# The shared expert's fifth token tile ahead of the routed loop, and ScalarE makes the statistics of three tiles of the second norm

## The chip, the cores and the metric

The kernel runs on one core of one Trainium2 chip. A core has TensorE (PE, matmuls), VectorE (DVE), ScalarE (ACT) and GpSimd (POOL), and SyncE (SP), which issues DMAs; the engines run their own instruction streams and meet by semaphores. The metric is the time of one execution on the device in microseconds; several executions are timed and the median counts.

## What is computed

One layer of a decoder trunk for 1024 tokens of width 1024: a token mixer with four branches, a layer norm, a mixture of experts, a second layer norm. The change touches the shared expert of the mixture and the second norm.

```python
def layer_norm(x, g, b):
    mu = jnp.mean(xf, -1, keepdims=True)
    var = jnp.mean(jnp.square(xf - mu), -1, keepdims=True)
    return ((xf - mu) * lax.rsqrt(var + LN_EPS) * g + b).astype(x.dtype)
...
# moe_ffn: 64 experts of width 256, 6 of them per token, rows sorted by expert in blocks of 128
h = xpad[tok]
y = (jax.nn.silu(h @ wg[e]) * (h @ wu[e])) @ wd[e]
...
shared = (jax.nn.silu(xt @ sh_wg) * (xt @ sh_wu)) @ sh_wd
x = layer_norm(ALPHA * x + (routed + shared), ln2_g, ln2_b)
```

## The kernel before

The tokens lie in NT = 8 tiles of 128 rows. The last half of the program (the function back) has three stages that matter here.

**Ahead of the routed loop.** The first norm makes x1 of every tile, TensorE turns it (turn_x1), the router is computed, and then TensorE makes the shared expert of the first NU = 4 tiles. For one tile t that is: shared_up(t), 8 matmuls of 128x512 for gate and up together; ScalarE's silu and a copy of the up half (shared_gated); GpSimd's product of both (shared_hidden, L1552); TensorE turns the product (shared_turn, L1663); ScalarE copies the turned product out (L1964); TensorE's shared_down (4 matmuls, L1672); ScalarE empties the banks (L1974); GpSimd adds ALPHA * x1 (L1582) and stores the sum as the tile's rows of acc in HBM (L1584). s_y counts the tiles whose banks are empty. SyncE waits for s_y to reach NU before it loads the weights of experts 2 and 3. The other tiles' rows of acc are ALPHA * x1 alone.

**The routed loop.** 76 blocks, each of up to 128 rows of one expert: gather by GpSimd, turn, up (L1704 and L1700 to L1702), down (L1719, 12 matmuls), and a scatter with addition to acc (even blocks) or acc_odd (odd blocks).

**The last stage.** Behind the last routed down product TensorE makes the shared expert of tiles 4 to 7 (shared_up at L1652, tail_turn at L1779, tail_down at L1790), one tile's up product ahead of the turn and down product of the tile before. ScalarE makes the silu (tail_gated, L1988) and copies the turned product (tail_turned, L1993), VectorE the product (tail_hidden, L2282). SyncE reads the eight tiles of acc into SBUF (L1523), GpSimd reads acc_odd on top of them with an adding DMA (L1615), and odd_in[t] tells that tile t is complete. Then the second norm, tile by tile: for tiles 4 to 7 VectorE adds the shared expert's two halves from the banks (L2315, it counts s_y up); VectorE makes the statistics of the two halves (L2319) and puts them together (L2321); ScalarE takes the root (deviation, L2033); VectorE's three 128x1 instructions (scales, L2298 to L2300) make scale and shift; ScalarE applies them (normal, L2037); VectorE multiplies by the gain g2 (gain, L2304); GpSimd adds the offset b2 (L1619); SyncE stores the tile. tail_down(6) and (7) wait for the banks that VectorE's addition of tiles 4 and 5 empties. The order of all this on each engine is written out by hand; nothing schedules it.

## Time and profile before

| | us |
|---|---|
| median of 3 runs | 2075.33 |
| lowest and highest | 2073.94, 2077.75 |
| the profiled execution | 2077.22 |
| its span, first to last instruction | 2075.4 |

The profile is of one execution. Its page gives TensorE as busy for 2010.3 us (97% of the span), VectorE for 1350.9 (65%), ScalarE for 859.5 (41%), GpSimd for 553.1 (27%). The shares are means over stages with different limits; what one stage is worth is read from its own rows. A row of the timeline has the start, the duration, the engine, the line, what it writes and reads, and in brackets the idle time ahead and what ended it. The chain of waits follows the work that ended last back from the last instruction; its rows are start, duration, engine, tile and line.

### The profile page before, as it was taken

How to read it: one execution, taken by the hardware profiler on the slowest of the kernel's cores; microseconds unless marked ns; L12 is line 12 of the kernel's file. 1: busy time of each engine (PE TensorE's matmuls, PEld its weight loads, DVE VectorE, ACT ScalarE, POOL GpSimd, SP SyncE). 2: the span in 40 equal slices, each digit the busy share in tenths (PEclk: the TensorE clock that was granted, in tenths of full speed). 3: DMA queues.
4: the chain of work that ended last, by engine and by line, in shares of the span. 5: the costliest groups of instructions: out<-in, count | busy, mean ns of one | idle time of the engine just before them, and what ended most of it. 6: DMA issues, size and time to landing. Idle time of an engine off the chain costs nothing.

```text
span 2075.4 us, 33282 instructions
## 1 busy us (share of the span) xinstructions
PE 2010.3 (97%) x9805; PEld 1448.0 (70%) x9806; DVE 1350.9 (65%) x2797; ACT 859.5 (41%) x1446; POOL 553.1 (27%) x366
## 2 busy tenths in 40 slices
PE   8999999999999999989999999999999999999995
PEld 7887787877778766668667457666667776666762
DVE  2894543344026777788667657777777777777756
ACT  2111221344112344430133256656666666666643
POOL 2342231323322211012120132223222222332224
PEclk9999999999999999999999999999999999999998
DMA  6122221222622210158551488899898989899856
GB/s 199 51 67 92 76 61 31 82 56 62 168 66 82 64 47 27 43 202 294 195 226 44 171 323 292 309 350 337 319 327 277 358 292 331 311 312 305 298 169 184
DMA packets 167747, 389.07 MB, mean 187 GB/s; under 512 B 26193, under 2 KB 98162, under 8 KB 142961
## 3 DMA queue, kind: packets, MB, share of 16 engines
q1 hardware_dynamic: 129696, 298.02, 39.4%
q0 software_dynamic: 28752, 73.18, 14.1%
q10 hardware_dynamic: 9216, 16.78, 2.2%
q8 instruction: 50, 0.82, 0.2%
q14 instruction: 33, 0.26, 0.0%
HBM read 337.04 MB, written 80.22 MB: 201 GB/s over the span
## 4 chain that ended last, share of the span: by engine, by line
PE 40%; DMA 6%; issue 2%; DVE 2%; ACT 1%; ACTq 0%; DVEq 0%; POOLq 0%
PE e_bank L1704 9%; PE e_bank L1719 9%; DMA work<-x1d,idx 6%; PE e_bank L1682 3%; PE e_bank L1634 3%; PE e_bank L1700 3%; PE e_bank L1652 3%; PE e_bank L1701 2%; PE e_bank L1702 2%; PE e_bank L1644 2%; PE e_bank L1672 1%; PE e_bank L1753 1%; PE e_bank L1790 1%; PE e_bank L1853 1%; PE e_bank L1731 1%
## 5 line engine op out<-in xcount | busy, mean ns | idle before, releaser
L646 PE MATMUL a_bank<-x_hi,w_hi 128*128 128x512 f32 x928 | 373.2, 402 | 0.0
L646 PE MATMUL a_bank<-x_hi,w_lo 128*128 128x512 f32 x928 | 362.7, 391 | 0.0
L646 PE MATMUL a_bank<-x_lo,w_hi 128*128 128x512 f32 x928 | 361.8, 390 | 0.0
L1704 PE MATMUL e_bank<-w_gu,work 128*128 x616 | 277.2, 593 | 2.1 <-issue 1.4
L2236 DVE TENSOR_TENSOR d_lo<-w_d,d_hi 128x1024 fp32r<-128x1024 f32 x152 | 180.8, 1230 | 61.2 <-ACT d_hi L2001 61.1
L581 POOL CAST w_hi<-w_raw 128x1024 fp32r<-128x1024 f32 x56 | 64.7, 1156 | 560.2 <-PE a_bank L646 539.5
L646 PEld LDWEIGHTS a_bank<-x_hi,w_hi 128*128 128x128 f32 x928 | 174.4, 188 | 40.5 <-issue 6.1
L646 PEld LDWEIGHTS a_bank<-x_hi,w_lo 128*128 128x128 f32 x928 | 174.2, 188 | 37.7
L646 PEld LDWEIGHTS a_bank<-x_lo,w_hi 128*128 128x128 f32 x928 | 174.7, 188 | 33.9 <-issue 0.5
L1704 PEld LDWEIGHTS e_bank<-w_gu,work 128*128 128x128 f32 x616 | 111.9, 192 | 113.3 <-issue 113.3
L1900 ACT ACTIVATE u_hi<-w_gu 128x1024 fp32r x150 | 159.0, 1061 | 2.0 <-POOL work L1582 1.7
L2001 ACT ACTIVATE d_hi<-w_d 128x1024 fp32r x152 | 152.3, 1049 | 5.6 <-issue 3.7
L583 POOL TENSOR_TENSOR w_lo<-w_raw,w_hi 128x1024 fp32r<-128x1024 f32 x56 | 145.4, 2596 | 4.6
L1905 ACT ACTIVATE norm<-e_bank 128x256 f32<-128x256 f32 x76 | 29.2, 384 | 252.3 <-PE e_bank L1702 248.5
L1598 POOL DMA_INDIRECT acc<-work,idx_out x38 | 80.2, 2111 | 197.5 <-issue 191.3
L1542 POOL DMA_INDIRECT work<-x1d,idx x77 | 81.4, 1057 | 181.0 <-DVE idx L2201 169.6
L1598 POOL DMA_INDIRECT acc_odd<-work,idx_out x38 | 74.7, 1966 | 202.7 <-DVE idx_out L2257 189.2
L1719 PE MATMUL e_bank<-d_hi,h_hi 128*128 128x512 f32 x304 | 126.0, 414 | 0.0
L1700 PE MATMUL e_bank<-u_hi,x_g_hi 128*128 128x512 f32 x300 | 124.8, 416 | 0.0
L874 ACT ACTIVATE gate_out<-a_bank 128x512 f32<-128x512 f32 x64 | 38.2, 597 | 204.7 <-PE a_bank L646 204.5
L1719 PE MATMUL e_bank<-d_hi,h_lo 128*128 128x512 f32 x304 | 120.5, 397 | 0.0
L1719 PE MATMUL e_bank<-d_lo,h_hi 128*128 128x512 f32 x304 | 119.3, 392 | 0.0
(378 smaller groups left out, 3867.1 us busy)
## 6 DMA issues: line engine op xcount, KB each, us to landing
w_gu<-in_moe_wg SPq DMA_DIRECT2D x64, 1024.0 KB
w_gu<-in_moe_wu SPq DMA_DIRECT2D x64, 1024.0 KB
w_d<-in_moe_wd SPq DMA_DIRECT2D x64, 1024.0 KB, 12.5
w_raw<-in_w_in SPq DMA_DIRECT2D x53, 512.0 KB, 3.8
gates<-gate_out ACTq DMA_DIRECT2D x64, 256.0 KB, 2.0
g_sb<-gates SPq DMA_DIRECT2D x16, 1024.0 KB, 5.3
acc_odd<-zero POOLq DMA_DIRECT2D x9, 512.0 KB, 13.3
work<-in_w_out SPq DMA_DIRECT2D x4, 1024.0 KB, 8.8
```

Source lines behind the costliest of these rows:

```text
L581: pool.tensor_copy(w_hi[:, c % 2, :, :], w_raw[:, c % 2, :, :]).then_inc(w_hi_ready, 1)
L583: pool.tensor_tensor(w_lo[:, c % 2, :, :], w_raw[:, c % 2, :, :], w_hi[:, c % 2, :, :].bitcast(F32), ALU.subtract).then_inc(w_lo_ready, 1)
L646: ins = pe.matmul(bank[h][:, :], w[:, c % 2, k, :], x[:, k, cols], start=(k == 0 and j == 0), stop=(k == KD - 1 and j == 2))
L1542: pool.indirect_dma_start(out=x_g[:, s, :], out_offset=None, in_=x1d[:, :], in_offset=bass.IndirectOffsetOnAxis(ap=idx[:, s:s + 1], axis=0 ...
L1598: pool.indirect_dma_start(out=(acc, acc_odd)[s][:, :], out_offset=bass.IndirectOffsetOnAxis(ap=idx_out[:, s:s + 1], axis=0), in_=y_out[:, ...
L1634: pe.matmul(bank[2 * (t % 2) + h][:, :], merged[:, k, rows], w_out[:, k, h * HALF:(h + 1) * HALF], start=k == 0, stop=False)
L1700: pe.matmul(out, hi, u_hi[:, j, :, i, :], start=False, stop=False)
L1704: ins = pe.matmul(out, x_gt[:, s, k, :], w_gu[:, bass.ds(e & 3, 1), :, k, :].rearrange('p a m f -> p (a m) f'), start=k == 0, stop=k == KD ...
L1719: ins = pe.matmul(bank[2 + h][:, :], x[:, j, :], w[:, j, cols], start=j == 0 and i == 0, stop=j == 1 and i == 2)
L1900: act.activation(up_part(u_hi[:, j, :, :, :]), up_weights(slot, j), ACT.Copy).then_inc(u_hi_ready, 1)
L2001: act.activation(d_hi[:, j, :], w_d[:, bass.ds(e & 3, 1), j, :].rearrange('p a f -> p (a f)'), ACT.Copy).then_inc(d_hi_ready, 1)
L2236: dve.tensor_tensor(d_lo[:, j, :], w_d[:, bass.ds(slot, 1), j, :].rearrange('p a f -> p (a f)'), d_hi[:, j, :].bitcast(F32), ALU.subtract) ...
```

## The change

NM = 5 tiles now have their shared expert made ahead of the routed loop, and the last stage has it for tiles 5 to 7. SyncE, ScalarE, GpSimd and TensorE go by NM where they went by NU; only tiles 5 to 7 have plain ALPHA * x1 rows in acc. In the second norm the tiles 0, 2 and 4 (BY_ACT) get their statistics from ScalarE: a copy of the tile onto itself with the row sums as a second output, VectorE makes the mean of it (one 128x1 instruction), and ScalarE squares the difference to the mean with the sums of squares as a second output (row_sums). The root takes those sums with a scale of 1/D. The other five tiles keep VectorE's statistics. The order of the last stage is new on TensorE, ScalarE and VectorE; the silu of tile 7 now stands ahead of all norms.

```diff
 NU = NT // 2
+NM = NU + 1
+BY_ACT = (0, 2, 4)
...
         m_lo = nc.alloc_sbuf_tensor_at('m_lo', [P, 4, S], F32R, offset=work_at + 4 * 4 * S)
+        squares = w_gu[:, 2, 0, 0:4, :].rearrange('p k f -> p (k f)')
         g2, b2 = (w_gu[:, 1, 1, 4 * i:4 * i + 4, :].rearrange('p k f -> p (k f)') for i in range(2))
...
         scale, shift = sb('ln2_scale', [P, NT]), sb('ln2_shift', [P, NT])
+        sums = sb('ln2_sums', [P, NT, 2])
+        row_sum, row_mean, squared = sem('row_sum'), sem('row_mean'), sem('squared')
...
             load_down(1, 1)
-            for t in range(NU, NT):
-                sp.wait_ge(x_scaled, t - NU + 1)
+            for t in range(NM, NT):
+                sp.wait_ge(x_scaled, t - NM + 1)
                 sp.dma_start(acc[t * P:(t + 1) * P, :], x1_n[:, t, :]).then_inc(acc_rest, 16)
...
             down_landed(0, 0)
-            sp.wait_ge(s_y, NU)
+            sp.wait_ge(s_y, NM)
             load_up(2, 2)
...
             load_down(3, 3)
-            sp.wait_ge(acc_rest, 16 * (NT - NU))
+            sp.wait_ge(acc_rest, 16 * (NT - NM))
             load_up(3, 3)
...
             shared_hidden(0)
-            for t in range(NU):
+            for t in range(NM):
                 s = t % 2
-                if t + 1 < NU:
+                if t + 1 < NM:
                     shared_hidden(t + 1)
...
             for s in range(2):
-                pool.wait_ge(acc_in[s], 16 * NU // 2)
-            pool.wait_ge(acc_rest, 16 * (NT - NU))
+                pool.wait_ge(acc_in[s], 16 * ((NM + 1 - s) // 2))
+            pool.wait_ge(acc_rest, 16 * (NT - NM))
             n = trips(pool)
...
                 for k in range(KD) if part is None else range(4 * part, 4 * part + 4):
-                    ins = pe.matmul(bank[s][:, :], turned_x1(t)[:, k, :], (s_gu if t < NU else tail_gu)[:, k, :], start=k == 0,
+                    ins = pe.matmul(bank[s][:, :], turned_x1(t)[:, k, :], (s_gu if t < NM else tail_gu)[:, k, :], start=k == 0,
                                     stop=k == KD - 1)
...
                 pe.wait_ge(s_ht_out, t + 1)
-                if t >= NU + 2:
+                if t >= NM + 2:
                     pe.wait_ge(s_y, t - 1)
...
             shared_turn(2)
+            shared_up(4)
             shared_down(2)
...
             shared_down(3)
-            pe.wait_ge(s_ht_out, NU)
+            shared_turn(4)
+            shared_down(4)
+            pe.wait_ge(s_ht_out, NM)
             turn(0, 0, 16)
...
                 up(0, 0, e_first[0], part)
-            pe.wait_ge(s_y, NU)
+            pe.wait_ge(s_y, NM)
...
                     pe.wait_ge(tail_in, 48)
-                    shared_up(NU)
+                    shared_up(NM)
                 if ahead1:
...
             body(2 * n + 1, 1, n, ahead1=False, ahead=False)
-            shared_up(5)
-            tail_turn(4)
-            pe.wait_ge(y_act, 2 * n + 3)
-            tail_down(4)
             shared_up(6)
             tail_turn(5)
+            pe.wait_ge(y_act, 2 * n + 3)
             tail_down(5)
...
             act.wait_ge(x1_stored, 16 * NT)
-            for t in range(NU):
+            for t in range(NM):
                 s = t % 2
...
                                ).then_inc(s_ht_out, 1)
-                if t + 1 < NU:
+                if t + 1 < NM:
                     shared_gated(t + 1)
-                act.activation(x1_n[:, NU + t, :], x1_n[:, NU + t, :], ACT.Copy, scale=ALPHA).then_inc(x_scaled, 1)
+                if t < NT - NM:
+                    act.activation(x1_n[:, NM + t, :], x1_n[:, NM + t, :], ACT.Copy, scale=ALPHA).then_inc(x_scaled, 1)
                 if t >= 2:
...
             e_one = expert_of(act, 1)
-            act.wait_ge(s_acc_ready, NU)
+            act.wait_ge(s_acc_ready, NM)
             act.wait_ge(gu_landed, e_one + 1)
...
                 else:
-                    tail_gated(NU)
+                    tail_gated(NM)
                 if ahead:
...
+            def row_sums(t):
+
+                act.wait_ge(odd_in[t], 16)
+                act.activation(rows2[:, t, :], rows2[:, t, :], ACT.Copy, accum_out=sums[:, t, 0:1]).then_inc(row_sum, 1)
+                act.wait_ge(row_mean, BY_ACT.index(t) + 1)
+                act.activation(squares, rows2[:, t, :], ACT.Square, scale=-1.0, bias=mv[:, t % 2, 0:1],
+                               accum_out=sums[:, t, 1:2]).then_inc(squared, 1)
+
             def deviation(t):
-                act.wait_ge(mv_done2, t + 1)
-                act.activation(sd[:, t % 2:t % 2 + 1], mv[:, t % 2, 1:2], ACT.Sqrt, bias=eps[:, 0:1]).then_inc(sd_done2, 1)
+                if t in BY_ACT:
+                    act.wait_ge(squared, BY_ACT.index(t) + 1)
+                    act.activation(sd[:, t % 2:t % 2 + 1], sums[:, t, 1:2], ACT.Sqrt, scale=1.0 / D, bias=eps[:, 0:1]
+                                   ).then_inc(sd_done2, 1)
+                else:
+                    act.wait_ge(mv_done2, sum(i not in BY_ACT for i in range(t + 1)))
+                    act.activation(sd[:, t % 2:t % 2 + 1], mv[:, t % 2, 1:2], ACT.Sqrt, bias=eps[:, 0:1]).then_inc(sd_done2, 1)
...
                                bias=shift[:, t:t + 1]).then_inc(normed, 1)
-            tail_gated(5)
-            tail_turned(4)
-            act.wait_ge(s_h, NU + 1)
             tail_gated(6)
             tail_turned(5)
+            act.wait_ge(s_h, NM + 1)
+            tail_gated(7)
+            tail_turned(6)
+            row_sums(0)
             deviation(0)
...
             normal(0)
+            act.wait_ge(s_down, NM + 1)
+            tail_turned(7)
+            normal(1)
+            row_sums(2)
             deviation(2)
-            normal(1)
             deviation(3)
             normal(2)
-            act.wait_ge(s_h, NU + 2)
-            tail_gated(7)
-            act.wait_ge(s_down, NU + 1)
-            tail_turned(6)
-            act.wait_ge(s_down, NU + 2)
-            tail_turned(7)
+            normal(3)
+            row_sums(4)
             for t in range(4, NT):
                 deviation(t)
-                normal(t - 1)
+                if t > 4:
+                    normal(t - 1)
             normal(NT - 1)
...
             body(2 * n + 1, 1, n, ahead1=False, ahead=False)
-            dve.wait_ge(ht_done, 2 * n + 3)
-            tail_hidden(4)
             dve.wait_ge(ht_done, 2 * n + 4)
             tail_hidden(5)
-            dve.wait_ge(s_ht, NU + 1)
             tail_hidden(6)
+            dve.wait_ge(s_ht, NM + 1)
+            tail_hidden(7)
...
                 s = t % 2
-                if t == 5:
-                    dve.wait_ge(s_ht, NU + 2)
-                    tail_hidden(7)
-                dve.wait_ge(odd_in[t], 16)
-                if t >= NU:
+                if t not in BY_ACT:
+                    dve.wait_ge(odd_in[t], 16)
+                if t >= NM:
                     dve.wait_ge(s_down, t + 1)
...
                     dve.wait_ge(s_y, t + 1)
-                for h in range(2):
-                    ins = dve.bn_stats(stats[:, s, h, :], rows2[:, t, h * HALF:(h + 1) * HALF])
-                X(ins)
-                dve.bn_aggr(mv[:, s, :], stats[:, s, :, :]).then_inc(mv_done2, 1)
-                if t:
-                    scales(t - 1)
+                if t in BY_ACT:
+                    if t:
+                        scales(t - 1)
+                    dve.wait_ge(row_sum, BY_ACT.index(t) + 1)
+                    dve.tensor_scalar(mv[:, s, 0:1], sums[:, t, 0:1], 1.0 / D, None, ALU.mult).then_inc(row_mean, 1)
+                else:
+                    for h in range(2):
+                        ins = dve.bn_stats(stats[:, s, h, :], rows2[:, t, h * HALF:(h + 1) * HALF])
+                    X(ins)
+                    dve.bn_aggr(mv[:, s, :], stats[:, s, :, :]).then_inc(mv_done2, 1)
+                    if t:
+                        scales(t - 1)
                 if t >= 2:
```

TensorE ahead of the loop, from the up product of tile 3 to the first transposes of the loop (sh holds the shared weights, norm and work_49 the turned products, x and x_late the turned x1). Before:

```order
L1652 MATMUL e_bank<-sh,x 128x512 x4
L1672 MATMUL e_bank<-sh,work_49 128x512 x4
L1663 MATMUL e_bank<-e_const,norm 128x128 x2
L1672 MATMUL e_bank<-sh,norm 128x512 x4
L1663 MATMUL e_bank<-e_const,norm 128x128 x2
L1672 MATMUL e_bank<-sh,work_49 128x512 x4
L1682 MATMUL e_bank<-e_const,work_49 128x128 x8
```

And after:

```order
L1657 MATMUL e_bank<-sh,x 128x512 x4
L1677 MATMUL e_bank<-sh,work_49 128x512 x4
L1668 MATMUL e_bank<-e_const,norm 128x128 x2
L1657 MATMUL e_bank<-sh,x_late 128x512 x8
L1677 MATMUL e_bank<-sh,norm 128x512 x4
L1668 MATMUL e_bank<-e_const,norm 128x128 x2
L1677 MATMUL e_bank<-sh,work_49 128x512 x4
L1668 MATMUL e_bank<-e_const,norm 128x128 x2
L1677 MATMUL e_bank<-sh,norm 128x512 x4
L1687 MATMUL e_bank<-e_const,work_49 128x128 x8
```

The up product of tile 4 (x_late, L1657) stands between the turn and the down product of tile 2, and its turn and down product are a third pair behind the two.

ScalarE at the start of the second norm: from the copy of tile 5's turned product (before) and tile 6's (after). The rows with ln_sd are roots, those with ln_shift normalizations. Before:

```order
L1993 ACTIVATE norm<-e_bank 128x256
L2033 ACT_TABLE_LOAD
L2033 ACTIVATE ln_sd<-ln_mv,b_eps 128x1 x2
L2037 ACTIVATE x<-x,ln_shift,ln_scale 128x1024
L2033 ACTIVATE ln_sd<-ln_mv,b_eps 128x1
L2037 ACTIVATE x<-x,ln_shift,ln_scale 128x1024
L2033 ACTIVATE ln_sd<-ln_mv,b_eps 128x1
L2037 ACTIVATE x<-x,ln_shift,ln_scale 128x1024
L1988 ACT_TABLE_LOAD
L1988 ACTIVATE norm<-e_bank 128x256
L1993 ACTIVATE norm<-e_bank 128x256 x2
L2033 ACT_TABLE_LOAD
```

And after:

```order
L1999 ACTIVATE norm<-e_bank 128x256
L2040 ACTIVATE x,ln_sums<-x 128x1024
L2042 ACTIVATE w_gu,ln_sums<-x,ln_mv 128x1024
L2048 ACT_TABLE_LOAD
L2048 ACTIVATE ln_sd<-ln_sums,b_eps 128x1
L2052 ACTIVATE ln_sd<-ln_mv,b_eps 128x1
L2056 ACTIVATE x<-x,ln_shift,ln_scale 128x1024
L1999 ACTIVATE norm<-e_bank 128x256
L2056 ACTIVATE x<-x,ln_shift,ln_scale 128x1024
L2040 ACTIVATE x,ln_sums<-x 128x1024
L2042 ACTIVATE w_gu,ln_sums<-x,ln_mv 128x1024
L2048 ACTIVATE ln_sd<-ln_sums,b_eps 128x1
```

The silu with its table load is gone from the middle; the two passes of tile 0 and of tile 2 (ln_sums) stand ahead of the roots.

VectorE in the same stage, from the gain of tile 0 on. Before:

```order
L2304 TENSOR_TENSOR x<-x,w_gu 128x1024
L2319 BN_STATS ln_stats<-x 128x6 x2
L2321 BN_AGGR ln_mv<-ln_stats 128x2
L2298 RECIPROCAL ln_sd<-ln_sd 128x1
L2299 SCALAR_TENSOR_TENSOR ln_shift<-ln_mv,ln_sd 128x1
L2300 COPY ln_scale<-ln_sd 128x1
L2304 TENSOR_TENSOR x<-x,w_gu 128x1024
L2315 TENSOR_TENSOR x<-x,e_bank 128x512 x2
L2319 BN_STATS ln_stats<-x 128x6 x2
L2321 BN_AGGR ln_mv<-ln_stats 128x2
L2298 RECIPROCAL ln_sd<-ln_sd 128x1
```

And after:

```order
L2323 TENSOR_TENSOR x<-x,w_gu 128x1024
L2342 BN_STATS ln_stats<-x 128x6 x2
L2344 BN_AGGR ln_mv<-ln_stats 128x2
L2317 RECIPROCAL ln_sd<-ln_sd 128x1
L2318 SCALAR_TENSOR_TENSOR ln_shift<-ln_mv,ln_sd 128x1
L2319 COPY ln_scale<-ln_sd 128x1
L2323 TENSOR_TENSOR x<-x,w_gu 128x1024
L2317 RECIPROCAL ln_sd<-ln_sd 128x1
L2318 SCALAR_TENSOR_TENSOR ln_shift<-ln_mv,ln_sd 128x1
L2319 COPY ln_scale<-ln_sd 128x1
L2339 TENSOR_SCALAR ln_mv<-ln_sums 128x1
L2323 TENSOR_TENSOR x<-x,w_gu 128x1024
```

Before, statistics stand between each of these gains and the next scale block; after, the scale block of tile 3 comes straight behind the gain of tile 1, and the mean of tile 4 (which waits for ScalarE) behind that.

## Rows read from the trace of the kernel before

**Rows 1.** Chain of waits, ahead of and in the loop: start, us, what.
```profile
1193.19 3.69 PE e_bank L1672 x8
...
1198.40 3.67 PE e_bank L1672 x8
...
1242.35 2.78 PE e_bank L1719 x12
...
1252.72 2.78 PE e_bank L1719 x12
...
2001.56 2.73 PE e_bank L1719 x12
```

**Rows 2.** Timeline, TensorE and GpSimd ahead of the loop.
```profile
1191.48 0.38 PE L1663 MATMUL e_bank<-e_const,norm 128*128 128x128 f32 x2
...
1196.11 0.74 POOL L1552 TENSOR_TENSOR norm<-norm 128x256 f32<-128x256 f32 x1
...
1198.06 2.36 POOL L1582 TENSOR_TENSOR work<-work 128x1024 f32<-128x1024 f32 x1 [1.20 <-ACT work L1974]
...
1200.71 0.57 POOL L1584 DMA_DIRECT2D acc<-work  x1 [0.30 <-POOL work L1582]
```

**Rows 3.** Chain of waits in the last stage.
```profile
2025.49 6.88 PE e_bank L1652 x16
...
2045.82 5.40 PE e_bank L1790 x8
...
2051.94 1.28 ACT L2033
```

**Rows 4.** Timeline of the last stage, ScalarE, VectorE and GpSimd.
```profile
2032.74 0.38 ACT L1993 ACTIVATE norm<-e_bank 128x256 f32<-128x256 f32 x1
...
2047.47 1.27 DVE L2315 TENSOR_TENSOR x<-x,e_bank 128x512 f32<-128x512 f32 x2
...
2055.83 1.28 DVE L2315 TENSOR_TENSOR x<-x,e_bank 128x512 f32<-128x512 f32 x2
...
2060.01 1.28 DVE L2315 TENSOR_TENSOR x<-x,e_bank 128x512 f32<-128x512 f32 x2
...
2061.33 1.29 DVE L2319 BATCH_NORM_STATS2 ln_stats<-x 128x6 f32<-128x512 f32 x2
...
2063.06 1.22 DVE L2304 TENSOR_TENSOR x<-x,w_gu 128x1024 f32<-128x1024 f32 x1
...
2064.35 2.34 POOL L1619 TENSOR_TENSOR x<-x,w_gu 128x1024 f32<-128x1024 f32 x1 [1.82 <-DVE x L2304]
2064.38 2.32 DVE L2299 SCALAR_TENSOR_TENSOR ln_shift<-ln_mv,ln_sd 128x1 f32<-128x1 f32 x1
```

**Rows 5.** Busy time by stretch of the last stage; PEclk is the granted clock.
```profile
core 0: us, PE busy (x) PEld busy (x) DVE busy (x) ACT busy (x) POOL busy (x), PEclk, DMA share, GB/s
...
2043.00:2052.00 9.00, 6.60 (x15) 2.62 (x13) 7.13 (x16) 2.57 (x6) 4.71 (x2) 0.81 0.92 270
```

**Rows 6.** ScalarE's groups of instructions by form: count, busy us, mean ns.
```profile
L989 ACT ACTIVATION_READ_ACCUMULATOR reg_s<-reg_s,m_neg 128x1 f32 x80 | 15.1, 188 | 0.0
...
L2037 ACT ACTIVATE x<-x,ln_shift,ln_scale 128x1024 f32<-128x1024 f32 x8 | 9.9, 1236 | 3.2 <-DVE ln_scale L2300 3.2
...
L1943 ACT ACTIVATE x<-x 128x1024 f32<-128x1024 f32 x8 | 8.3, 1043 | 0.0
...
L989 ACT ACTIVATE reg_s<-reg_s,m_neg 128x1024 f32<-128x1024 f32 x3 | 3.4, 1141 | 0.0
...
L2033 ACT ACTIVATE ln_sd<-ln_mv,b_eps 128x1 f32<-128x1 f32 x8 | 2.3, 292 | 8.4 <-DVE ln_mv L2321 8.4
```

**Rows 7.** The adding reads of acc_odd (L1615): starts, and us to landing.
```profile
L1615 POOL DMA_DIRECT2D x<-acc_odd x8: 955/1564/2775, 2024.8 to 2029.1; - x8
...
DMA to landing us min/median/max: 5.9/12.2/20.4
```

**Rows 8.** The stores of acc ahead of the loop (L1584): us to landing.
```profile
DMA to landing us min/median/max: 2.9/3.1/9.1
```

## The prediction

> **What bounds the kernel now.** I read three views, in this order. First the chain of waits that ended last, for the stretch that the change lengthens: ahead of the routed loop the chain lies on TensorE, one down product after the other (L1672, 3.67 us each, a new one every 1198.40 - 1193.19 = 5.21 us), then through the loop, and at its far end on TensorE again [rows 1, 3]. Then the timeline of the three engines that hand the fourth shared tile around ahead of the loop [rows 2]. Then the timeline and the chain of the last stage: TensorE still makes the shared expert of tiles 4 to 7 there, one 128x512 up product of 6.88 us and one down product per tile; ScalarE reloads a table (1.28 us) after TensorE's last one; and only then does VectorE take the rows of tiles 6 and 7 and finish [rows 3, 4]. VectorE's steady step per tile is 2060.01 - 2055.83 = 4.18 us, and from its addition for tile 7 (2060.01) to the end of the span (2075.4) it is 15.4 us. But 2055.83 - 2047.47 = 8.36 us lie between the additions of tiles 5 and 6: 4.18 of them are waiting for ScalarE, which stood behind TensorE. So the last stage loses some 4.2 us to TensorE, not the 11 us that TensorE spends on a tile. That is the first thing to see.
>
> **The profiled execution and the median.** The span of the profiled execution is 2075.4 us, the execution with what lies around it 2077.22, the median 2075.33. I work out differences of the span and put them on the median.
>
> **Part 1: the fifth tile ahead of the loop.** TensorE gets shared_up(4) between shared_turn(2) and shared_down(2), and shared_turn(4), shared_down(4) behind shared_down(3). Before, turn(2) starts at 1191.48 and down(2) at 1193.19, the turn itself 0.38: 1.33 us of idling, in which ScalarE empties the banks of down(1) [rows 1, 2]. The up product (6.88 by the same shape in the last stage) fills that gap: down(2) moves from 1193.19 to about 1191.9 + 6.9 = 1198.8, so 5.6 us later. Then one more period of down products: 5.2 us. Is that period kept? down(3) would start at 1204.0 and end at 1207.5; turn(4) needs GpSimd's product of tile 4 (hidden), which the new code puts behind the addition and the store of tile 2. In the rows of tile 2 the addition starts 1198.06 - 1193.19 = 4.87 us behind down(2) and takes 2.36; the store comes 2.65 us after the addition's start and takes 0.57, the product 0.74 [rows 2]. From 1198.8 that gives 1203.7, 1206.3, 1206.9 and 1207.7: a wait of 0.2 us at most. down(4) then starts at 1209.2 and the loop's first transposes, first up product and SyncE's loads of experts 2 and 3 (they wait for s_y, now 5) all stand 10.8 us later. Loads, gathers and GpSimd's last waits are shifted along with TensorE, so none of them hides it. ScalarE's copy of x for tile 4 waits for tile 2's store, issued at 1206.9: with 3.1 us it lands at 1210.0, and down(4) ends at 1212.9, so it is covered; with 9.1 us, the longest of its kind [rows 8], it would come at 1216, and 3 us would be added. **Sum of part 1: +10.8 us**, from 10.3 (no wait at all) to 13.8.
>
> **Part 2: the routed loop.** Its code is the same. It isn't free of waits: from the down product at 1242.35 to that at 2001.56 there are 72 blocks, 10.54 us each, where two undisturbed ones lie 1252.72 - 1242.35 = 10.37 apart [rows 1]. So 72 x 0.17 = 12 us of waiting lie in it, for gathers by the chain. Nothing moves a gather against the weight loads around it. I take 0, and +-1.5 us for scatter, since the three runs lie 3.8 us apart.
>
> **Part 3: the last stage.** TensorE loses one up product, two transposes and a down product there: 6.88 + 0.4 + 3.67, some 11 us. Its order is up(6), turn and down(5), up(7), ..., so up(7) stands where up(6) stood, ending at 2032.37 [rows 3]. Up to there nothing moves: ScalarE turns to the norm at 2032.74 + 0.38 = 2033.1, as before [rows 4]. From here the end hangs on VectorE and ScalarE, so I lay their new orders beside each other. Prices [rows 6]: a plain copy of 128x1024 is 1.04 us, an activation with a bias column and accumulator 1.14, reading the accumulator out 0.19, the normalization 1.24, a square root 0.29, a table load 1.28 [rows 3]; neighbours on ScalarE overlap by 0.1. VectorE in its steady step [rows 4]: addition 2061.33 - 2060.01 = 1.32, statistics and scale block 2063.06 - 2061.33 = 1.73 (I give the block of three 128x1 instructions 0.3 of it), gain the rest of 4.18, 1.13 until the next one starts.
> - Tile 0: copy 2033.05 to 2034.2, VectorE's mean 2034.4, square to 2035.6, table to 2036.9, roots of tiles 0 and 1 to 2037.35, VectorE's scales to 2037.55, normalization of tile 0 to 2038.85, the turned tile 7 to 2039.1, normalization of tile 1 to 2040.25.
> - Tile 2: copy to 2041.3, mean, square to 2042.7, root to 2043.05. VectorE waits for the copy, then gain(0) to 2042.6 and the statistics of tile 3 to 2044.05.
> - Now GpSimd. A VectorE instruction with two tiles of SBUF as input doesn't run beside GpSimd's addition of 2.34 us: the shift of tile 7 (128x1) starts at 2064.38, 0.03 us after GpSimd's addition, and takes 2.32 us [rows 4]. This comes about where a gain is followed at once by a scale block. The new order has that twice among the first five tiles: the shift of tile 2 meets the addition of tile 0 (2042.7 to 2045.0; it would have started at 2044.1, so 0.9 us), and the shift of tile 3 comes straight behind gain(1) (to 2046.25), and stands until 2048.7 (2.35 us).
> - ScalarE then: normalization of tile 3 to 2050.0, copy of tile 4 to 2051.1. VectorE, which waits for it: mean, gain(2) to 2052.4, and the addition of tile 5 starts at 2052.3, not at 2047.47.
> - From there VectorE has its steady 4.18 us per tile, without the stall of 4.2: tile 6 at 2056.5, tile 7 at 2060.65, end at 2060.65 + 15.4 = 2076.05, against 2075.4. The last two collisions with GpSimd stay as they are.
> TensorE's down product of tile 7 waits for the addition of tile 5, so it runs from 2053.6. At full clock it takes 3.67 us; one that lay in a stretch with a mean granted clock of 0.81 (part of it at 1.2 GHz and not at 2.4) took 5.40 [rows 3, 5], and all of it at 1.2 GHz would be 7.3: to 2060.9, against 2060.65 wanted. So it is hidden, or costs 0.3.
> The three statistics of VectorE that are taken away (3 x 1.4 us) and the addition of tile 4 (1.32) thus buy nothing, as VectorE waits for ScalarE's two passes in a row. **Sum of part 3: +0.6 us**. The unknown prices are the copy with accumulator (1.04 to 1.24 us, and from 0 to 0.19 for the read-out) and the two hand-overs per tile (0.05 to 0.2): +-0.4 per tile, so -1.2 to +1.2. Without the two collisions it would be 0.6 - 3.25 = -2.6.
>
> **The table load, a rule against a row.** Here ScalarE's silu for tile 7, between two loads before, is gone, so one load less and no return: the row shows 1.28 us, and the root behind it follows at once [rows 3]. The Trainium skill, "ScalarE: Activation LUTs", section "What ACT_TABLE_LOAD costs", adds a drain of about 1.38 us to each switch; by that the remaining load would cost 1.4 us more and the sum would be +12.8; the trace doesn't show that drain.
>
> **The rivals.**
> - *VectorE's own work decides.* The statistics on ScalarE run beside VectorE's work and the stall goes as well. Then the addition of tile 5 is bound by its rows: the eight reads of acc_odd start at 2024.8, the first lands after 5.9, the last (2029.1) after 20.4 us, at 2049.5 [rows 7], which makes the sixth about 2044.1 in even steps. End 2044.1 + 2 x 4.18 + 15.4 = 2067.9, -7.5; with +10.8 that is +3.3: 2078.6, **not slower** by the bound below. It decides if the addition of tile 5 starts before 2045. For it: VectorE has 5.6 us less to do. Against: the two passes per tile, each with a hand-over to VectorE and back, lie in front of VectorE's next step. The Trainium skill, "Perfetto Trace Analysis", section "Optimizing Scalar/DVE Operations", says that offloading from a saturated VectorE to ScalarE may make sense; that rule stands for this rival.
> - *TensorE's chain sets the end to the last.* The end follows it by all of 11 us, and a table load of 1.28: -12.3 + 10.8 = -1.5: 2073.8. Against: rows that land at 2049.5 can't leave by 2063.
> - *No collisions* in the first five tiles: 2075.33 + 10.8 - 2.6 = 2083.5. It needs GpSimd's additions 0.1 us later than in the row at 2064.35.
> - *The late store* of part 1: 2086.7 + 3 = 2089.7.
> - *The fifth tile hidden*: the loop's gather waits (12 us) take it up, and the time stays near 2076. Nothing in the trace speaks for it.
>
> **How the numbers follow.** Forecast: 2075.33 + 10.8 + 0 + 0.6 = **2086.7 us**, chance 0.66. No collisions 0.16, late store 0.09, VectorE's own work 0.04, TensorE's chain 0.02, hidden 0.02, and 0.01 for the last two together, which alone would be faster (-12.3 us). The range takes in no collisions with 1 us of scatter and the late store: 2082.5 to 2090.0. Of this kernel 0.2%, 4.2 us, can be told from no change. Slower by more: 0.91; within: 0.08 (VectorE's own work, TensorE's chain, hidden); faster: 0.01.
>
> **What would show it.** Right: the first up product of the loop 10 to 12 us later; up(4) in the place of the idling before down(2); in the last stage VectorE waiting for ScalarE at tiles 0, 2 and 4, a shift of about 2.3 us before the addition of tile 5, that addition near 19 us after ScalarE turned to the norm, and 4.2 us, not 8.4, from it to the addition of tile 6. Wrong: the addition of tile 5 within 12 us of that point, or a loop whose start moved by less than 9 us.

## The result, and the profile after

The changed kernel takes **2090.82 us** (median of 5 runs, 2087.18 to 2092.73). The kernel before, timed beside it, has 2077.33 (5 runs, 2073.94 to 2080.4). The ratio is 1.0065 with a 95% interval of 1.0049 to 1.0081, so the change costs 13.5 us, with some 10 to 17 in the interval. It is slower, as forecast, but 2090.82 lies 0.8 us above the range that the prediction gave, and 4.1 above its 2086.7. In the last of the three series of timings below some executions of both kernels took some 60 us longer, and the medians are of the others.

Cut at four points that both kernels have, the two profiled executions differ as follows. The second half begins with its first TensorE instruction; the turn of tile 2 is the one at 1191.48 in [rows 2]; the loop is taken from its first up product to the end of its last down product.

| us | before | after | difference | forecast |
|---|---|---|---|---|
| start to second half | 1021.59 | 1023.96 | +2.4 | 0 |
| to the turn of tile 2 | 169.89 | 170.22 | +0.3 | 0 |
| to the loop's first up product | 13.02 | 23.51 | +10.5 | +10.8 |
| routed loop | 809.62 | 809.90 | +0.3 | 0 |
| last stage, to the end | 61.28 | 62.11 | +0.8 | +0.6 |
| span | 2075.4 | 2089.7 | +14.3 | +11.4 |

The two stretches that the change touches came out at 11.3 us for 11.4 forecast. The rest of the 14.3 us between these two executions lies in stretches that it doesn't touch, and most of that ahead of 1024 us.

First the page of after, its head and its busy times:

```profile
span 2089.7 us, 33286 instructions
...
PE 2013.4 (96%) x9805; PEld 1449.2 (69%) x9806; DVE 1348.1 (65%) x2788; ACT 865.5 (41%) x1459; POOL 556.9 (27%) x369
```

VectorE lost three tiles' statistics and an addition and is 2.8 us less busy, ScalarE is 6.0 us busier. Neither number shows where 13 us went: both engines are idle for more than a third of the span.

The chain of waits in the stretch ahead of the loop (start, us, what), which answers to [rows 1]:

```profile
1194.56 6.87 PE e_bank L1657 x16
1201.43 3.45 PE e_bank L1677 x8
...
1206.41 3.69 PE e_bank L1677 x8
...
1211.62 3.67 PE e_bank L1677 x8
...
1217.69 4.55 PE e_bank L1709 x10
```

And the timeline of the engines there (start, us, engine, line, what it writes and reads, and in brackets the idle time ahead with what ended it), which answers to [rows 2]:

```profile
1201.27 3.60 PE L1677 MATMUL e_bank<-sh,norm 128*128 128x512 f32 x8
...
1206.06 2.35 POOL L1587 TENSOR_TENSOR work<-work 128x1024 f32<-128x1024 f32 x1 [6.51 <-ACT work L1980]
...
1208.70 0.58 POOL L1589 DMA_DIRECT2D acc<-work  x1 [0.30 <-POOL work L1587]
1209.30 0.74 POOL L1557 TENSOR_TENSOR norm<-norm 128x256 f32<-128x256 f32 x1
...
1210.09 0.44 PE L1668 MATMUL e_bank<-e_const,norm 128*128 128x128 f32 x2
...
1211.66 1.06 ACT L1977 ACTIVATE work<-x 128x1024 f32<-128x1024 f32 x1 [0.19 <-DMA acc<-work]
```

What to see: the up product of tile 4 (L1657, 6.87 us) stands directly ahead of the down product of tile 2, with no idling left between them; then the down products of tiles 3 and 4 follow at 1206.41 and 1211.62, 5.1 and 5.2 us apart. GpSimd comes to the product of tile 4 at 1209.30, behind its addition and its store, and is done at 1210.04; the transposes that read it start at 1210.09, right behind the down product of tile 3, which ended at 1210.08. So it arrives just in time. The store issued at 1208.70 has landed by 1211.66, before the last down product ends: it costs nothing.

The last stage, ScalarE from the moment at which it turns to the norm, which answers to the chain and the copy in [rows 3, 4]:

```profile
2046.48 1.06 ACT L2040 ACTIVATE x<-x 128x1024 f32<-128x1024 f32 x1
2047.42 0.20 ACT L2040 ACTIVATION_READ_ACCUMULATOR x<-x 128x1 f32 x1
...
2049.18 1.28 ACT L2048 ACT_TABLE_LOAD   x1
2050.47 0.29 ACT L2048 ACTIVATE ln_sd<-ln_sums,b_eps 128x1 f32<-128x1 f32 x1
...
2062.49 1.24 ACT L2056 ACTIVATE x<-x,ln_shift,ln_scale 128x1024 f32<-128x1024 f32 x1 [2.38 <-DVE ln_scale L2319]
```

And VectorE, GpSimd and TensorE beside it:

```profile
2047.73 0.15 DVE L2339 TENSOR_SCALAR ln_mv<-ln_sums 128x1 f32<-128x1 f32 x1 [0.89 <-ACT x L2040]
...
2050.80 0.16 DVE L2317 RECIPROCAL ln_sd<-ln_sd 128x1 f32<-128x1 f32 x1 [1.48 <-ACT ln_sd L2048]
...
2054.97 0.15 DVE L2339 TENSOR_SCALAR ln_mv<-ln_sums 128x1 f32<-128x1 f32 x1 [3.42 <-ACT x L2040]
...
2057.75 1.01 DVE L2318 SCALAR_TENSOR_TENSOR ln_shift<-ln_mv,ln_sd 128x1 f32<-128x1 f32 x1
...
2060.06 2.33 DVE L2318 SCALAR_TENSOR_TENSOR ln_shift<-ln_mv,ln_sd 128x1 f32<-128x1 f32 x1
...
2064.80 0.15 DVE L2339 TENSOR_SCALAR ln_mv<-ln_sums 128x1 f32<-128x1 f32 x1 [2.35 <-ACT x L2040]
...
2066.00 1.28 DVE L2332 TENSOR_TENSOR x<-x,e_bank 128x512 f32<-128x512 f32 x2
...
2070.17 1.28 DVE L2332 TENSOR_TENSOR x<-x,e_bank 128x512 f32<-128x512 f32 x2
...
2074.35 1.28 DVE L2332 TENSOR_TENSOR x<-x,e_bank 128x512 f32<-128x512 f32 x2
```

```profile
2056.41 2.34 POOL L1624 TENSOR_TENSOR x<-x,w_gu 128x1024 f32<-128x1024 f32 x1 [10.68 <-DVE x L2323]
2060.04 2.33 POOL L1624 TENSOR_TENSOR x<-x,w_gu 128x1024 f32<-128x1024 f32 x1 [1.29 <-DVE x L2323]
...
2067.42 5.22 PE L1795 MATMUL e_bank<-w_gu,norm 128*128 128x512 f32 x8 [16.86 <-DVE x L2332]
```

VectorE's waits for ScalarE are 0.89, 1.48, 3.42 and 2.35 us, at the tiles 0, 2 and 4 whose statistics ScalarE makes. The shift of tile 2 (128x1) takes 1.01 us and that of tile 3 takes 2.33: each ends as GpSimd's addition beside it ends (2056.41 + 2.34 = 2058.75, 2060.04 + 2.33 = 2062.37). From the turn to the norm (2046.48) to the addition of tile 5 (2066.00) it is 19.5 us; after that VectorE has its step of 4.17 us twice, where before there were 8.36 and 4.18 [rows 4].

### The profile page after: what moved, and what is told of

Its sections match the earlier page's. It is cut to its first block, busy times and chain, and to the rows that moved or that the text cites. A ratio compares the mean times of both kernels' runs of the same rounds, so it can differ in the third digit from the quotient of the medians.

```text
span 2089.7 us, 33286 instructions
## 1 busy us (share of the span) xinstructions
PE 2013.4 (96%) x9805; PEld 1449.2 (69%) x9806; DVE 1348.1 (65%) x2788; ACT 865.5 (41%) x1459; POOL 556.9 (27%) x369
## 3 DMA queue, kind: packets, MB, share of 16 engines
q0 software_dynamic: 28896, 73.71, 14.1%
## 4 chain that ended last, share of the span: by engine, by line
PE 38%; DMA 7%; DVE 2%; issue 2%; ACT 1%; ACTq 0%; DVEq 0%; POOLq 0%
PE e_bank L1709 9%; PE e_bank L1724 8%; DMA work<-x1d,idx 7%; PE e_bank L1687 3%; PE e_bank L1639 3%; PE e_bank L1657 3%; PE e_bank L1705 2%; PE e_bank L1706 2%; PE e_bank L1707 2%; PE e_bank L1649 2%; PE e_bank L1677 1%; PE e_bank L1758 1%; ACT d_hi L2007 1%; PE e_bank L1861 1%; PE e_bank L1736 0%
## 6 DMA issues: line engine op xcount, KB each, us to landing
w_gu<-in_moe_wu SPq DMA_DIRECT2D x64, 1024.0 KB, 12.4
```

## The experiments

Every kernel below computes the whole result. Ratios are to the kernel before, timed on the same chip in the same series of executions; a ratio is worked out from single executions and can differ a little from the quotient of two medians.

### The changed kernel again, and the kernel before again

Is the difference of 13.5 us itself firm, and what does a kernel of the same instructions give? Two of these are the changed kernel and one is the kernel before, with no instruction edited, so there is no diff to show.

> The changed kernel, unchanged, once more. Theory 1 (11.3 us of the 14.3 us between the two spans are the change: 10.5 from the turn of tile 2 to the loop's first up product, 0.8 from the last routed down product to the end; 2.5 us arise in code ahead of the second half that is the same in both, and are scatter): 11 to 12 us above the kernel before (ratio 1.0054 to 1.0058), and in its trace the second half starts within 2 us of 1020 on either side, not bound to 1022.6. Rival 1 (the 2.5 us belong to the change, by another placement of code or buffers): 13 to 14.5 us above, and the second half starts at 1022.5 again. Both: the stretch ahead of the loop 23.5 us long (13.0 before), the last stage 62.1 us (61.3 before).

> The kernel before once more, to see the scatter of executions: ratio 1.000 within 0.1%, the start of the second half anywhere from 1020.6 to 1025 us, early where TensorE's granted clock stays at 1.00 between 890 and 900 us and late where it falls to about 0.5 there.

> The changed kernel a third time. Theory 1: 11.3 us above the kernel before by its stretches (10.5 ahead of the loop, 0.8 in the last stage); with the two measurements so far (13.5 and 14.1, each some 3 us wide) the mean should go down to 12 or 13. Rival 1 (some 2.5 us more belong to the change, outside those stretches): 13.5 to 14 again.

| | median us | ratio to before (95%) | as us |
|---|---|---|---|
| changed kernel, first timing | 2090.82 | 1.0065 (1.0049 to 1.0081) | 13.5 |
| changed kernel again | 2091.71 | 1.0068 (1.0054 to 1.0082) | 14.1 |
| changed kernel, third time | 2088.25 | 1.0052 (1.0037 to 1.0067) | 10.8 |
| kernel before against itself | 2080.0 | 1.0008 (0.9993 to 1.0024) | 1.7 |

The last two rows are of one series (3 and 4 executions).

The same instructions differ by 1.7 us from themselves in one series, and the changed kernel by 3.3 us between series. The kernel before ran 16 times in the series of the second row: 2074.71 to 2080.81, median 2076.69. The median of 2075.33, on which the forecast stood, is in the lower third of them. The stretches say where this comes from:

| us | second half starts | to the turn of tile 2 | to the loop | loop | last stage |
|---|---|---|---|---|---|
| before | 1021.59 | 169.89 | 13.02 | 809.62 | 61.28 |
| before again | 1025.12 | 170.58 | 12.99 | 810.32 | 61.29 |
| after | 1023.96 | 170.22 | 23.51 | 809.90 | 62.11 |
| after again | 1020.65 | 170.26 | 23.52 | 809.99 | 62.08 |
| after, third time | 1025.29 | 169.59 | 23.51 | 808.30 | 62.11 |

The columns of the changed stretches agree within 0.03 us per kernel. The first column scatters by 4.6 us with no relation to the kernel, and the loop by 2.

Of the expectations for these three runs, the two stretches came out in all of them. The first repetition gave 14.1 us, which is the range of its rival (13 to 14.5), but its second half started at 1020.65, as the theory had it; the third timing gave 10.8 and a mean of 12.8, as the theory had it. The repetition of the kernel before missed: it starts its second half late, at 1025.12, with no lower clock between 890 and 900 us. The last section shows what made it late.

### The second norm's statistics back on VectorE, the fifth tile kept

This separates the two parts of the change, and tells the prediction's walk through the last stage from the rival in which VectorE's own work decides: if VectorE is what the stage waits for, giving it three more tiles of statistics makes it slower.

```diff
-BY_ACT = (0, 2, 4)
+BY_ACT = ()
...
-            row_sums(0)
...
+            deviation(2)
             normal(1)
-            row_sums(2)
-            deviation(2)
...
-            normal(3)
-            row_sums(4)
...
-                if t > 4:
-                    normal(t - 1)
+                normal(t - 1)
```

ScalarE's root of tile 2 goes back ahead of the normalization of tile 1 as well, as in the kernel before, so what is measured is the passes with their order.

> The changed kernel with the shared expert of five tiles ahead of the loop, but all statistics of the second norm on VectorE again (BY_ACT empty). Theory 1 (ScalarE's two passes per tile stand in front of VectorE's next step and cost more than they take off it): the last stage falls from 62.1 to about 56 us (gain and statistics of tiles 0 to 4 in steps of 3.7 us, set by GpSimd's addition, the addition of tile 5 some 13.5 us after ScalarE turns to the norm instead of 19.5), total 5.5 to 7 us below the changed kernel, 5 to 6 above the one before. Rival 2 (VectorE's own work decides, the passes on ScalarE are help): the last stage gets longer, by up to 3 x 1.4 us, to 66.

Median 2083.72 us, ratio 1.003 (1.0018 to 1.0042). The last stage takes 56.12 us, against 62.11 with ScalarE's passes: **6.0 us less, with more work on VectorE**. (By the medians of this series it is 8.0 us less than the changed kernel's 2091.71, where 5.5 to 7 were expected; the stage is the finer measure.) VectorE's additions of tiles 5 and 6 and the two shifts ahead of them, from the timeline of this kernel:

```profile
2053.00 1.01 DVE L2313 SCALAR_TENSOR_TENSOR ln_shift<-ln_mv,ln_sd 128x1 f32<-128x1 f32 x1
...
2056.71 0.94 DVE L2313 SCALAR_TENSOR_TENSOR ln_shift<-ln_mv,ln_sd 128x1 f32<-128x1 f32 x1
...
2058.77 1.27 DVE L2327 TENSOR_TENSOR x<-x,e_bank 128x512 f32<-128x512 f32 x2
...
2062.94 1.28 DVE L2327 TENSOR_TENSOR x<-x,e_bank 128x512 f32<-128x512 f32 x2
```

The last routed down product ends at 2026.28 in this kernel, so the addition of tile 5 comes 32.5 us behind it; in the changed kernel it is 2066.00 - 2027.60 = 38.4. From there both have 4.17 us per tile. The passes thus cost 5.9 us, all before the addition of tile 5, and the shift of 2.33 us (here 0.94) is 1.4 of them. VectorE is busy here for 13.16 of the 13.47 us from 2045.30 to 2058.77, without a wait for ScalarE; in the changed kernel it is busy for 11.19 of the 19.52 us from the turn to the norm to the addition of tile 5. This kernel has the fifth tile ahead of the loop and no passes: its last stage is 5.2 us shorter than before and its front some 10.5 longer, so the fifth tile alone is a loss too.

### The scale block of tile 3 ahead of the gain of tile 1

What are the collisions with GpSimd worth? Here one of them is taken away by order alone: the shift of tile 3 is made before VectorE has handed tile 1 to GpSimd. The passes stay on ScalarE.

```diff
-                    if t:
+                    if t and t != 4:
                         scales(t - 1)
...
+                    if t == 3:
+                        scales(3)
```

> The changed kernel with one block of three 128x1 instructions moved on VectorE: the scale block of tile 3 ahead of the gain of tile 1 instead of behind it. Theory 1 (that block stands 2.3 us for GpSimd's addition, and ScalarE and with it the addition of tile 5 wait for it): the shift of tile 3 takes 0.2 us instead of 2.33, the last stage 59.8 us instead of 62.1. Rival: the addition of GpSimd only blocks the next instruction with two inputs instead, the gain, and the last stage stays at 62.

Median 2085.5 us, ratio 1.004 (1.0027 to 1.0054). Last stage 59.82 us, 2.3 less than 62.11. VectorE's timeline:

```profile
2059.04 1.01 DVE L2318 SCALAR_TENSOR_TENSOR ln_shift<-ln_mv,ln_sd 128x1 f32<-128x1 f32 x1
...
2060.22 0.16 DVE L2318 SCALAR_TENSOR_TENSOR ln_shift<-ln_mv,ln_sd 128x1 f32<-128x1 f32 x1
...
2065.01 1.27 DVE L2332 TENSOR_TENSOR x<-x,e_bank 128x512 f32<-128x512 f32 x2
```

The second shift falls from 2.33 to 0.16 us, and the end comes 2.3 us earlier: that step of the walk lay on the path to the end in full. The medians can't show so small a step: in this series they are 6.2 us apart (2085.5 and 2091.71), and the profiled execution of this kernel took 2090.53.

### The passes alone, without the fifth tile

The kernel before, with ScalarE's statistics for tiles 0 and 2, and TensorE still making tile 4 in the last stage. The prediction has the stall of 4.2 us at tile 6 go because TensorE has a tile less to do there, not because VectorE has less to do; this tells the two apart.

```diff
+BY_ACT = (0, 2)
...
             tail_turned(5)
+            row_sums(0)
             deviation(0)
...
+            normal(1)
+            row_sums(2)
             deviation(2)
-            normal(1)
...
```

The function row_sums and VectorE's part are those of the change.

> The kernel before (four shared tiles ahead of the loop) with ScalarE's two passes for the statistics of tiles 0 and 2 and nothing else of the change. Theory 1 (the passes stand in front of VectorE's next step, and the stall behind TensorE stays): the stretch ahead of the loop 13.0 us as before, the last stage about 64 us (61.3 before), so 2 to 3 us above the kernel before. Rival 2 (taking statistics off VectorE shortens what it has to do): the last stage 61.3 us or less.

Median 2080.64 us, ratio 1.0014 (1.0 to 1.0028), so the whole time hardly tells it from the kernel before. Front 12.99 us, as before; last stage 65.00, **3.7 more** than before, though two tiles' statistics are taken off VectorE. The stall stands there still: VectorE waits 3.83 us for the root (3.26 in the kernel before), and the additions of tiles 5 and 6 lie 8.96 us apart (8.36 before):

```profile
2050.32 1.28 DVE L2335 TENSOR_TENSOR x<-x,e_bank 128x512 f32<-128x512 f32 x2
...
2057.00 0.17 DVE L2317 RECIPROCAL ln_sd<-ln_sd 128x1 f32<-128x1 f32 x1 [3.83 <-ACT ln_sd L2050]
...
2059.28 1.28 DVE L2335 TENSOR_TENSOR x<-x,e_bank 128x512 f32<-128x512 f32 x2
```

and ScalarE's timeline shows what it waits for, the transposes of TensorE (L1783), and the table load behind them:

```profile
2054.97 0.38 ACT L1997 ACTIVATE norm<-e_bank 128x256 f32<-128x256 f32 x1 [6.96 <-PE e_bank L1783]
2055.38 1.28 ACT L2050 ACT_TABLE_LOAD   x1
2056.67 0.30 ACT L2050 ACTIVATE ln_sd<-ln_mv,b_eps 128x1 f32<-128x1 f32 x1
```

So the passes lose time by themselves, and they do nothing for the stall. Of the 3.7 us, 3.2 are lost ahead of the addition of tile 5, which comes 36.5 us behind the last routed down product (33.35 before). The other 0.6 lie in the longer stall, where TensorE's down product of tile 6 took 6.59 us instead of 5.40; the mean granted clock was 0.62 from 2047 to 2056 us there.

### Only the order: ScalarE's copy of tile 7 behind two steps of the norm

If the stall is ScalarE standing behind TensorE's last transposes, it can be taken away without moving any work. The kernel before, with ScalarE's root of tile 4 and normalization of tile 3 ahead of its copy of tile 7's turned product:

```diff
             tail_turned(6)
+            deviation(4)
+            normal(3)
             act.wait_ge(s_down, NU + 2)
             tail_turned(7)
-            for t in range(4, NT):
+            for t in range(5, NT):
```

> The kernel before with one move on ScalarE in the last stage: the root of tile 4 and the normalization of tile 3 stand ahead of the copy of tile 7's turned product instead of behind it. Theory (the last stage of the kernel before loses only the stall between the additions of tiles 5 and 6, 8.4 us apart instead of 4.2, and that is ScalarE standing behind TensorE): these additions 4.2 us apart, the last stage 57.2 us instead of 61.3, total 4 us below the kernel before (ratio 0.998). Rival (TensorE's chain sets the end): the addition of tile 7 then waits for TensorE's last down product, ScalarE's copy comes up to 1.5 us later, and at most 2 us are gained.

Median **2073.37 us**, ratio 0.9983 (0.9974 to 0.9992), 11 executions: faster than both kernels. Last stage 57.05 us against 61.28. On ScalarE the table is loaded back without waiting, and the copy that waits for TensorE comes later and holds nobody up:

```profile
2046.72 1.28 ACT L2033 ACT_TABLE_LOAD   x1
2048.01 0.30 ACT L2033 ACTIVATE ln_sd<-ln_mv,b_eps 128x1 f32<-128x1 f32 x1
...
2050.77 0.38 ACT L1993 ACTIVATE norm<-e_bank 128x256 f32<-128x256 f32 x1 [1.33 <-PE e_bank L1779]
```

VectorE's additions of tiles 5 and 6 are then 4.17 us apart, not 8.36 [rows 4]; the last row is TensorE's down product of tile 6:

```profile
2048.40 1.27 DVE L2317 TENSOR_TENSOR x<-x,e_bank 128x512 f32<-128x512 f32 x2
...
2052.57 1.28 DVE L2317 TENSOR_TENSOR x<-x,e_bank 128x512 f32<-128x512 f32 x2
...
2046.75 3.70 PE L1790 MATMUL e_bank<-w_gu,norm 128*128 128x512 f32 x8 [1.87 <-ACT norm L1993]
```

One reservation: that down product takes 3.70 us in this execution, with a granted clock of 1.00, where it took 5.40 in both profiled executions of the kernel before, with 0.81 [rows 3, 5]. With 1.7 us more ScalarE's copy would end near 2052.9 and hold up the root of tile 5, which starts at 2051.27 (an estimate from these rows). So up to 1.6 of the 4.2 us can be the clock and not the order. The medians (3.5 us less, between 1.7 and 5.4) leave that open.

Most of what the last stage had to gain from TensorE's side is thus to be had for two lines that move, 2.6 to 4.2 us; the fifth tile paid 10.5 us for it.

### The up product of tile 4 not in the gap

The prediction credits the place of shared_up(4) with filling 1.33 us of idling, and keeps the period of the down products. Here it stands behind the down product of tile 3, with its turn behind it.

```diff
             shared_turn(2)
-            shared_up(4)
             shared_down(2)
...
             shared_down(3)
+            shared_up(4)
             shared_turn(4)
             shared_down(4)
```

> The changed kernel with the up product of tile 4 behind the down product of tile 3 instead of ahead of that of tile 2. Theory 1 (ahead of the loop everything lies on one chain; the change's place for the product fills 1.3 us of idling and covers silu and GpSimd's product): the stretch from the turn of tile 2 to the loop's first up product 26 to 27 us instead of 23.5. Rival (the stretch is bound by something beside that chain, such as the stores of acc or ScalarE's work): it stays at 23.5.

There is a single execution of it, of 2157.08 us, whose second half starts at 1088.37, so only the stretch counts: 26.56 us from the turn of tile 2 to the loop, against 23.51. TensorE's timeline:

```profile
1267.75 7.03 PE L1657 MATMUL e_bank<-sh,x_late 128*128 128x512 f32 x16
1276.34 0.44 PE L1668 MATMUL e_bank<-e_const,norm 128*128 128x128 f32 x2 [1.56 <-POOL norm L1557]
1277.82 3.67 PE L1677 MATMUL e_bank<-sh,norm 128*128 128x512 f32 x8 [1.04 <-ACT norm L1969]
```

Behind the up product TensorE now waits 1.56 us for the product of tile 4 to come round ScalarE and GpSimd, and the gap of 1.3 us ahead of the down product of tile 2 is open again; the whole stretch is 3.05 us longer. The place in the changed kernel is the good one; its 10.5 us are the work itself.

## Why the prediction was right, and where it failed

**The fifth tile ahead of the loop: right.** +10.8 forecast, +10.5 measured. The down product of tile 2 comes 1201.27 - 1194.18 = 7.09 us behind the turn, where it was 1.71 [rows 2]: 5.4 for 5.6 forecast. The added period is 5.2 for 5.2. The wait for GpSimd, bounded by 0.2, is 0.01 (1210.08 to 1210.09), and the store was covered, so the rival of the late store didn't come about. The timing without the gap shows the term by itself.

**The loop: right in its profile** (+0.3), and its scatter of 2 us over five executions is about the 1.5 either way that I gave it. Its own waits took nothing of the 10.5 up.

**The last stage: right, and for its reasons.** +0.6 forecast, +0.8 measured. From the turn to the norm to the addition of tile 5: 19.3 forecast (2033.05 to 2052.3), 19.5 measured. The two collisions: 0.9 and 2.35 forecast, 0.85 and 2.17 above the plain 0.16 measured, and taking the second away gave 2.3 us back. The stall: from 8.36 to 4.17 us between the additions of tiles 5 and 6. (Of the stall before, some 1.7 us came from the lower clock in the down product of tile 6, 5.40 against 3.67 us, an estimate; the prediction takes all of it as ScalarE standing behind TensorE's work.) From the addition of tile 7 to the end 15.4 and 15.35. The down product of tile 7 fell into a stretch with a lower clock, with 5.22 us, and was done at 2072.64, 1.7 us before the addition of tile 7 at 2074.35: hidden, as the first of the two bounds had it. VectorE's own work, the rival with -7.5 us for this stage, is refuted for the changed kernel: giving VectorE its statistics back made the stage 6.0 us shorter. Only in the kernel without the passes is VectorE what the stage waits for. "No collisions" is refuted by the two shifts. The sum over both edits was nearly zero only because a gain of 5.2 us (the stall, with its lower clock, and the addition of tile 4: 61.28 to 56.12) was eaten by 6.0 us of passes.

**The table load.** By the row it was 1.28 us with the next instruction right behind, and after shows the same: the load starts at 2049.18 and the root at 2050.47, 0.01 us behind its end. In the kernel with the later copy it is 2046.72 and 2048.01, 0.01 again. By the Trainium skill, "ScalarE: Activation LUTs", section "What ACT_TABLE_LOAD costs", each switch has a drain of about 1.38 us beside it; neither place has room for it, and the +12.8 that followed from it would put 1.4 us into a last stage that came out at +0.8.

**What failed: the base and the width.** The step is the one headed "How the numbers follow", with what "The profiled execution and the median" chose: I put the difference of 11.4 us on the median of three executions, 2075.33, as if that median were known exactly, and let the range end at 2090.0, which takes in the late store but hardly any scatter above it. Further timings of the same kernel have their medians at 2077.33 (5 executions, those three among them) and 2076.69 (16), so the base was 1.4 to 2.0 us low: from 2077.33 the same terms give 2088.7. The 2.1 us from there to 2090.82 are not in the stretches of the change, which came out at 11.3 for 11.4; they are scatter, or the open part below. A single execution ranges over 6 us (2074.71 to 2080.81). I gave +-1.5 us "for scatter, since the three runs lie 3.8 us apart", and to the loop alone; the stretch ahead of the second half, which I didn't look at because nothing changes in it, scatters by 4.6 us, where the range had 0.3 us above the late store for it. A range from 2083 to 2093 would have held every timing of the changed kernel's median (2088.25 to 2091.71).

**What stays open.** The terms sum up to 11.3 us in the profiles. The three comparisons gave 13.5, 14.1 and 10.8, each with about 3 us either way, so 11.3 lies in all three intervals; their mean is 12.8. If the changed kernel has another 1 to 2 us somewhere, it isn't in the stretches that it changes (they repeat within 0.03 us), and the runs are too few to find it in the loop or ahead of the second half. I don't settle that.

## What to carry to other kernels

Taking work off a busy engine helps only if the other engine has it done when the first one needs it: lay both orders beside each other, and don't go by the busy share. In the second norm of the kernel before (2033.0 to 2075.4 us) VectorE was busy for 35.0 of 42.4 us (83%) and ScalarE for 16.9 (40%), which looks like room. But the statistics of a tile are 1.4 us on VectorE, and on ScalarE two passes with hand-overs, 2.7 us for tile 0 (2046.48 to 2049.15), in a row ahead of VectorE's next step. VectorE then stood waiting for 0.89 + 1.48 + 3.42 + 2.35 = 8.1 us, and the stage was 6 us longer. The Trainium skill, "Perfetto Trace Analysis", section "Optimizing Scalar/DVE Operations", says that offloading may make sense if VectorE is saturated; at 83% in this stage it was near that, and the offloading still lost time.

A stall of one engine behind another is often one of order: before moving 11 us of matmuls to another stage, see whether the waiting instruction can stand two places later on its queue. And a prediction of some 10 us on 2000 needs the scatter of the whole program in its range, from executions if there are enough, not only the unknown prices of the edit.

## What the runs showed of the hardware

**Where the scatter arises.** Nine of the ten profiled executions (all but that of the late up product) start the second half between 1020.62 and 1025.29 us, though the instructions up to there are the same. Two places make the difference. The first is TensorE's granted clock between 890 and 910 us. Windows of the changed kernel, and of the same kernel again, in this order (us, busy time of each engine with its instructions, granted clock, DMA share, GB/s):

```profile
890.00:895.00 5.00, 3.48 (x28) 2.41 (x28) 4.76 (x12) 3.07 (x6) 0.00 (x0) 0.79 1.07 375
895.00:900.00 5.00, 4.94 (x30) 2.91 (x28) 1.95 (x3) 1.04 (x3) 0.00 (x0) 0.52 0.35 91
```

```profile
890.00:895.00 5.00, 4.22 (x42) 2.90 (x42) 4.83 (x9) 2.70 (x5) 0.00 (x0) 1.00 1.08 356
895.00:900.00 5.00, 4.38 (x44) 2.83 (x44) 1.93 (x3) 2.39 (x4) 0.00 (x0) 1.00 0.14 37
```

In the first, TensorE works at nearly 1.2 GHz (0.52) through 895 to 900 us, with 30 matmuls where there are 44 at 2.4 GHz; the second half then starts at 1023.96. In the second there is no dip, and it starts at 1020.65. Over all nine, from one and the same matmul near 850 us to the start of the second half it is 170.2 to 170.3 us where the mean granted clock from 890 to 910 us is 1.00 (three executions), 171.5 where it is 0.91, 172.9 where it is 0.83 and 173.9 to 174.0 where it is 0.74 (four). So the dip goes with up to 3.9 us.

The second place is the first 26 us of the program. The repetition of the kernel before has no dip at 890 us, and still it is among the latest, at 1025.12: the matmul that starts at 25.62 us in the other execution starts at 30.36 in it. One early matmul, in the kernel before and in its repetition:

```profile
12.79 0.40 PE L646 MATMUL a_bank<-x_hi,w_lo 128*128 128x512 f32 x1
```

```profile
17.53 0.63 PE L646 MATMUL a_bank<-x_hi,w_lo 128*128 128x512 f32 x1
```

The repetition waited 2.19 and 2.07 us for the first loads of x (0.36 and 1.03 in the other execution), and its matmuls take 0.63 us for 0.40. The view of the granted clock reads 1.00 there, but in the changed kernel's execution the same matmuls take 0.63 us in a stretch at 0.50 (12.4 to 15.6 us), so I take it for the lower clock. What makes the clock fall in one execution and not in another of the same instructions, the runs don't show.

**The collision is a matter of operands and timing, not of size.** A 128x1 instruction of VectorE that reads two SBUF tiles stood for 2.33 us when it was issued just behind the start of GpSimd's addition, for 1.01 and 0.94 when it came part of the way through, and 0.16 beside none. Moving it by one place in its queue took 2.3 us off the end. An instruction with one input kept its time beside the same addition: the reciprocal of tile 2, at 2057.61, took 0.11 us. An addition that reads one tile in SBUF and one of TensorE's banks kept its time too: 1.28 us at 2066.00, with GpSimd's addition from 2066.16 to 2068.51.

The prediction had one row for this, the shift of 2.32 us in [rows 4], and inferred that the cost goes down to what is left of GpSimd's instruction. The kernel before already shows that, in the shift of tile 2, beside a GpSimd addition from 2039.49 to 2041.83:

```profile
2040.83 1.01 DVE L2299 SCALAR_TENSOR_TENSOR ln_shift<-ln_mv,ln_sd 128x1 f32<-128x1 f32 x1
```
